# Raw weight rows of the 64-row tile, one to two places further up in the load queue

## What is computed

```python
gate, up = jnp.split(h @ w_ffn_up, 2, axis=-1)      # w_ffn_up: 1024 x 5632
ffn = (jax.nn.silu(gate) * up) @ w_ffn_down          # w_ffn_down: 2816 x 1024, "the down product"
x = layer_norm(ALPHA * x + (1 + g2) * ffn, ln2_g, ln2_b)
```

## The kernel before

| rows | used ahead of step | in the queue behind the loads of step, before |
|---|---|---|
| 12, 13 / 14, 15 | 52 | 55 / 56 |
| 16, 17 / 18, 19 | 56 | 59 / 60 |
| 20, 21 | 60 | 63 |

## Time and profile before

### The profile page before, as it was taken

One profiled execution on the slowest core, in us unless ns is written; L12 is line 12 of the kernel. 1 busy time (PEld: TensorE's weight loads), 2 busy tenths in 40 slices (PEclk: granted clock), 3 DMA queues, 4 the chain that ended last, 5 costly groups with the idle time before them and its releaser, 6 DMA issues. The chain is left out here.

```text
span 1432.9 us, 29230 instructions
## 1 busy us (share of the span) xinstructions
PE 1372.2 (96%) x10652; PEld 1245.8 (87%) x10652; DVE 944.8 (66%) x1593; ACT 590.8 (41%) x1455; POOL 565.1 (39%) x645
## 2 busy tenths in 40 slices
PE   5999899989999999999999999999999999999887
PEld 4899899988988888788799999999999998877465
DVE  5527786774466666798788666656666557766378
ACT  6524344436465656534643333332333335433120
POOL 3888866871133323333232344344234424000121
PEclk8999999999999999999999999999999999999999
DMA  9431434334454453522234434445543468985784
GB/s 328 134 108 43 116 94 132 103 87 150 121 193 135 160 168 122 184 92 74 69 87 157 156 125 159 156 147 185 184 133 123 153 235 325 382 282 202 270 295 182
DMA packets 184409, 234.64 MB, mean 164 GB/s; under 512 B 17708, under 2 KB 118640, under 8 KB 184304
## 3 DMA queue, kind: packets, MB, share of 16 engines
q1 hardware_dynamic: 181424, 221.52, 47.8%
q10 hardware_dynamic: 2880, 11.72, 2.1%
HBM read 170.29 MB, written 61.73 MB: 162 GB/s over the span
## 5 line engine op out<-in xcount | busy, mean ns | idle before, releaser
L2259 PE MATMUL bank<-split 128*128 128x512 f32 x924 | 213.1, 391 | 5.2 <-DVE p1acc L2614 2.4
L2259 PEld LDWEIGHTS bank<-split 128*128 128x128 f32 x924 | 173.3, 188 | 48.8 <-issue 6.5
L2345 PE MATMUL bank<-Tlo,rh 128*128 128x272 f32 x640 | 184.7, 289 | 0.0
L2345 PE MATMUL bank<-Thi,rh 128*128 128x272 f32 x640 | 184.2, 288 | 0.0
L2345 PE MATMUL bank<-Thi,rl 128*128 128x272 f32 x640 | 184.0, 288 | 0.0
L305 PE MATMUL bank<-hT_hi,whi 128*128 128x384 f32 (+1 forms) x504 | 167.7, 333 | 2.1 <-DVE wlo L295 1.9
L305 PE MATMUL bank<-hT_hi,wlo 128*128 128x384 f32 (+1 forms) x504 | 165.9, 329 | 0.0
L305 PE MATMUL bank<-hT_lo,whi 128*128 128x384 f32 (+1 forms) x504 | 165.8, 329 | 0.0
L2345 PE MATMUL bank<-hT_lo,rh 128*128 128x272 f32 x480 | 138.5, 289 | 0.0
L2345 PE MATMUL bank<-hT_hi,rl 128*128 128x272 f32 x480 | 138.4, 288 | 0.0
L2345 PE MATMUL bank<-hT_hi,rh 128*128 128x272 f32 x480 | 137.9, 287 | 0.0
(11 more groups left out here) (450 smaller groups left out, 3353.1 us busy)
## 6 DMA issues: line engine op xcount, KB each, us to landing
wada<-w_ada SPq DMA_DIRECT2D x12, 2048.0 KB, 9.1
raw<-w_up SPq DMA_DIRECT2D x40, 512.0 KB, 5.0
wsum<-w_down SPq DMA_DIRECT2D x11, 1024.0 KB, 5.6
wt<-wsum SPq DMA_DIRECT2D x11, 1024.0 KB, 4.0
rW<-wt SPq DMA_DIRECT2D x44, 256.0 KB, 6.6
split<-split SPq DMA_DIRECT2D x22, 512.0 KB, 5.3
wraw<-w_in SPq DMA_DIRECT2D x21, 512.0 KB, 4.1
rows<-convrow ACTq DMA_DIRECT2D x16, 577.5 KB, 3.4
```

The source lines that it names most:

```text
L2259: last = pe.matmul(ps[down_bank(q, r)][:], a[:, rows], w, start=(k == 0 and m == 0), stop=(k == KH - 1 and m == 2))
L2345: last = pe.matmul(ps[banks[c]][:, 0:NC], w[:, ks], a, start=(n < 3 and k == 0 and p == 0), stop=(k == 3 and p == 2), skip_group_check=True)
```

## The change

Instead of one distance for all groups, each group of four (or two) has its own: 3 for the first three groups, 1 for those used ahead of steps 52 and 56, 2 for that ahead of step 60. The loads are the same in number, size and target, and so are all waits. Only their order in SP's queue changes.

```diff
-        X_LATER = 3
+        X_LATER = {Q7 * KH + 7: 3, Q4 * KH: 3, Q4 * KH + 4: 3, Q4 * KH + 8: 1, Q3 * KH + 1: 1, Q3 * KH + 5: 2}
         WHOLE = Q3 * KH
-        x_rows = lambda s: [b for at_, rows in HALF_ROWS.items() for n, b in enumerate(rows) if at_ + X_LATER + n // 2 == s]
+        x_rows = lambda s: [b for at_, rows in HALF_ROWS.items() for n, b in enumerate(rows) if at_ + X_LATER[at_] + n // 2 == s]
```

## The result

The changed kernel takes 1425.74 us (median of 6 runs, 1423.42 to 1426.54), the kernel before 1435.68 us (6 runs). The ratio is 0.9929 with a 95% interval of 0.9916 to 0.9941: 10.2 us faster (9.9 by the medians). The prediction was 1424.7 us and a gain of 11.05. Measured twice more, the changed kernel gave 0.9930 and 0.9922.

What follows compares the result with a forecast made beforehand. Bound: the rows' place in SP's queue, behind a load that waits for TensorE. Stalls of 12.94 us less 1.89 for the later DVE chain gave 11.05 us gain, so 1424.7 us, range 1422.2 to 1427.4.

Steps and rivals of the forecast that it cites:

- The stalls: TensorE's standing for late raw rows in the periods before steps 52, 56 and 60: 12.94 us, all to go.
- Row 13's hold: SP stands about 10 us at row 13 for row 8's buffer, delaying A54, W54 and W55; costed at nothing.
- the rival on the slower side: Hold at row 13 could make splits of step 54 and later some 16 us late: 1439 us; chance 0.03.
- W63 behind the rows: Rows 20, 21 ahead of W63 put its split 8.4 us after A62's issue, not 4.53; 1.89 us off the gain.
- The law behind it: DVE's chain runs from the start of the split of step 64 to L2614 in 19.97 us, before and after.
- the estimate of 6.2 us: Rival time for the four-transfer burst before W63, instead of 8.37 us: gain 13.2 us, time 1422.5; no separate chance.
- From L2614 to the end nothing changes: Behind the DVE instruction L2614, the way to the kernel's end was to take as long as before.
- The wait for the bank: TensorE's wait for the bank that L2614 frees was to grow from 2.4 to 4.3 us.

Runs made afterwards that it cites:

- only_12: Changed kernel with only rows 12 to 15 further up (distances of the last three groups 1, 3, 3); ratio to the kernel before 0.9955.
- not_20: Changed kernel with rows 20 and 21 left at distance 3 (last three groups 1, 1, 3); ratio to the kernel before 0.9918.
- only_20: Changed kernel with only rows 20 and 21 further up (last three groups 3, 3, 2); ratio to the kernel before 1.0003.
- again: The changed kernel measured once more, no edit; ratio to the kernel before 0.9930.
- again2: The changed kernel measured a third time, no edit; median 1424.60 us, ratio to the kernel before 0.9922.
- third: Changed kernel, with DVE freeing Q3's four banks ahead of stats_S and centred(4) instead of behind them; ratio to the kernel before 0.9925.
- spread: Changed kernel, with POOL doing tile 3's small steps before adding the sample tile instead of behind it; ratio to the kernel before 0.9901.
- both: Changed kernel with the two reorderings of third and spread together; ratio to the kernel before 0.9906.
- last1: Changed kernel with rows 20 and 21 at distance 1 instead of 2, ahead of W62 instead of W63; ratio to the kernel before 0.9879.
- last1_again: The kernel of last1 measured once more; median 1420.86 us, ratio to the kernel before 0.9901.

## Why the prediction was right, and where it was off

**The stalls** were read rightly in kind and size. 12.94 us were to go, 12.87 went; only_12 (6.5 us), not_20 (11.8) and the timelines of only_12 and only_20 show them to be separate, each going with its own group's place in the queue.

**Row 13's hold** was about as forecast, 11.2 us for the two issues. ACT then waited for W54 (a 5.92 us wait that ends with a DMA), but TensorE did not. Costing it at nothing was right, and the rival on the slower side had no part in it.

**W63 behind the rows** was to be split 8.4 us behind A62 and was 7.92 (7.79 in only_20, 7.92 to 9.30 in again, again2, third, spread and both). That rows 20 and 21 give their own gain away through DVE was the least obvious step. It is shown from both sides: only_20 gains nothing, and last1, which takes the rows out of W63's way, gains some 4 us more. The law behind it, L2614 some 20 us behind the split of step 64, held at 19.97 to 20.00 us in all ten profiled executions that leave the order at the end alone.

By the Trainium skill ("DMA: Bandwidth & Descriptors", "Anatomy of one DMA — SWDGE (gpsimd) path") a transfer by the gpsimd path costs about 2.0 us plus its bytes at 436 GB/s, which gave the estimate of 6.2 us for that burst. The loads here are issued by SP, and the executions with the rows ahead of W63 showed 7.79 to 9.30, so the estimate was too low for them.

**The step that failed** is "From L2614 to the end nothing changes". The wait for the bank was forecast to grow (4.3 us; it is 3.7), but it was priced at its length, and the clock behind it at nothing. Behind it the granted clock was 0.50 for 6 us, and 2.18 us were lost there. The rows had a warning: the prediction says itself that the clock fell where TensorE had stood, and in before it was 0.50 from 1336.0 to 1339.0, just behind the 2.48 us row wait that ended at 1335.53. The forecast of 11.05 us without that term, with the W63 term 0.5 us better, would have been 11.5. Less the clock's 2.2 and the 0.6 of the start of this execution it is the 8.7 of the profiled spans. The runs' 10.2 us lie between, as they would if the slow clock lasts differently long: the mean clock of the six runs ranges from 0.983 to 0.987, and the run with 0.987 took 1423.42 us, the shortest. That the clock cost is the whole difference in every run was not measured, and other things vary too: in again and again2, the same program, step 60 started at 1361.51 and 1360.01 us. So part of the closeness is luck. The profiled execution was forecast at 1423.6 us and took 1425.92; the W63 term's 0.5 us, and a profiled execution that this time lay above the median of the runs and not 1.14 under it, brought the median to within about 1 us.

By the Trainium skill ("TensorE: Matmul & The Clock Gate", "Part 1: The HAM clock gate (the "warmup" mystery)") TensorE has a slow and a fast state, and idleness brings the slow one back. The 0.50 behind the waits of 3.72 and 4.29 us agrees.

**The clock is not the last word on the end**: third had no slow clock and gained little, since DVE needs 33.1 us from the split of step 64 to its first tile of the end (33.06 in third, 33.07 in only_12, both without a wait for TensorE). With the rows ahead of W63 that split starts 1.7 to 3.1 us behind step 60. last1 starts it 0.6 us ahead of step 60, and that is what shortens the way from step 60 to that tile to 32.6.

## What to carry to other kernels

A load whose place in an in-order queue is behind one that waits for the consuming engine is late by construction. Look for an engine's waits on it, then find the gap in the issuing queue, and move it ahead of the waiting issue. But price what then stands behind it as well: the first load behind a burst is late by the burst, and it should be one that no serial chain hangs on. And a wait of TensorE may cost more than its length: at this bank all those of 3.26 us and more had a slower clock behind them.

## What the runs showed of the hardware

**The clock behind a wait.** Behind waits at the bank of 0.59, 1.38, 1.40, 1.75 and 2.04 us the mean granted clock was 1.00 over the next six microseconds; behind 2.41 twice 1.00, and behind 2.43 once 0.72; behind 3.26, 3.72, 3.73, 4.00 and 4.29 it was 0.72, 0.50, 0.72, 0.55 and 0.50. So near 2.4 us the same wait can go either way, and the same program with the same wait (3.72 and 3.73) had the slow level for the whole six microseconds or for part of them. Two shorter waits close together can have it too: behind 1.89 and 0.94 us the clock was 0.52 in both, and 1.00 behind 1.89 and 0.96 in third.

**DVE and POOL in each other's way.** In the changed kernel DVE runs ahead into POOL's additions at L2214, and three of its operations take 1 us longer than in before, where the same pair takes 0.68 and 1.29. DVE's timeline after, then POOL's:

```profile
1347.83 1.62 DVE L2388 TENSOR_TENSOR split<-rW,split 128x512 fp32r<-128x512 f32 x1
1349.37 2.38 DVE L2630 TENSOR_TENSOR u1acc<-u1acc,g2r 128x512 f32<-128x512 f32 x2
1351.68 1.78 DVE L2388 TENSOR_TENSOR split<-rW,split 128x512 fp32r<-128x512 f32 x1
```

```profile
1347.32 3.29 POOL L2214 TENSOR_TENSOR accA<-accA,u1acc 128x512 f32<-128x512 f32 x2 [119.03 <-DVE u1acc L2630]
1351.30 3.32 POOL L2214 TENSOR_TENSOR accA<-accA,u1acc 128x512 f32<-128x512 f32 x2 [0.69 <-DVE u1acc L2630]
```

The Trainium skill ("SBUF — State Buffer", "Who interferes with whom") has a DVE instruction with two inputs from SBUF contend with a GpSimd instruction that reads SBUF, and the order of issue decide which of them blocks. The rows agree: POOL's two pairs of additions take 3.3 us each, where they take 2.8 in before, so both engines are held in turn. The split of 2.90 us in spread agrees too. In the changed kernel DVE still has 2.06 us to wait for W63 behind them, so it costs nothing. In last1 DVE goes almost without a gap up to the split of step 64, but that split starts 0.03 us behind ACT's (done at 1360.73), which had waited for the landing of W64, and 0.28 us behind it in last1_again. So there it could cost 0.3 us at most; no run took it off.
